# Weight sums on VectorE at each turn's begin, and another order for putting the half-size results together

## The chip, the cores and the metric

One Trainium2 chip, one core. The metric is the device time of one execution in microseconds (us). Engines: PE (TensorE), DVE (VectorE), ACT (ScalarE), POOL (GpSimd), SP (SyncE, which issues the loads).

## The reference

Two transformer blocks of two layers each over 512 tokens of width 1024, in float32. Most of the time goes to six gated feed-forward networks (FFN) of hidden width 2816:

```python
def swiglu(h, w_gate, w_up, w_down):
    return (jax.nn.silu(h @ w_gate) * (h @ w_up)) @ w_down
x = x + 0.5 * swiglu(rms_norm(x, ffn1_norm[l]), ffn1_w_gate[l], ffn1_w_up[l], ffn1_w_down[l])
```

Between them lie convolutions, sparse attention, attention on a memory, retention and differential attention, which the change doesn't touch.

## The kernel before

Activations lie transposed: 128 channels on the partitions, 512 tokens along them. A float32 product is made of three passes over rounded halves: each weight tile `raw` (128x1024, one tile of 128 output columns) is rounded by ACT to `w_hi` (`round_weights`, line 1080) and DVE writes the rest to `w_lo` (`rest_of_weights`, line 1537); the activations are `u_hi` and `u_lo`, the hidden ones `h_hi` and `h_lo`. Weight tiles have running numbers and four slots; bank `n % 4` of PSUM takes tile n. SP loads a tile when the `w_lo` of the tile four before it is written (semaphore `split`), in the order of the numbers. `taken` counts tiles whose bank has been read by DVE.

An FFN (`ffn` of each engine) goes through its 22 hidden tiles in three groups of 8, 8 and 6 (`F_GROUPS`). A group computes gate and up tiles, then a down stage of eight tiles multiplies the group's hidden tiles into the residual. The gate and up work runs in turns of two hidden tiles. In a turn the first pair (tiles n and n+1) is plain: gate scaled by `rstd` (line 1643), tanh on ACT, up scaled (line 1647), (1 + tanh) times gate (line 1650), the product (line 1651), `h_hi` on ACT, `h_lo` on DVE (line 1541).

The second pair (n+2, n+3) is "quick" in 57 turns: the 2x2 block product of (gate, up) by (256-token halves) is made by a Winograd scheme with seven half-size products instead of eight, each 12 matmuls of 256 columns (`fast_pair`, line 588). Its products are m1, m2 (plain weights), then m5, m6, m3, m7 with weight sums S1, S2, S4, S3, and m4. The sums are made in `w_sum` from `raw` of n+2 and n+3 by POOL (`fast_sums`, line 2257), rounded by ACT to `sum_hi` (line 1123, 128x2048) and the rest written by DVE to `sum_lo` (`rest_of_sums`, line 1601). The token sums T1 to T4 are made once for an FFN by DVE (`summed`, lines 1609 to 1617). ACT copies m1 and m5 to `kept`; DVE puts the gate tile together in `fast_gate` (m2 and m3 plus `kept`, then m6 and m1 as `part_2` onto the second half) and the up tile in `fast_up`, from `part_3` (m7 plus `part_2`), `kept` and m4. Each tile is scaled by `rstd`.

Semaphores that matter: `s_made` counts sets of weight sums (ACT's rounding and SP's load of tile n+2 of the next turn, line 444, wait for it), `s_rounded` and `s_split` follow `sum_hi` and `sum_lo`, `w_mm` counts the four sum products of a pair (`w_mm` 5 to 8 of a turn), `f_ready` the `h_lo` tiles. POOL makes the sums of a turn in the turn before, behind `s_split` of that turn. `chain.done` makes an engine wait for its own instruction. The order of DVE's and ACT's work within a turn is the order of the calls in the loop (lines 1698 to 1712 and 1117 to 1137).

In the first FFN the first group is plain throughout. In the other five, the first group has three quick turns after a plain one, in which the norm of the tokens (`norm_scale`), the token sums and their splitting are made too.

Of the kernel before, what the change touches and what calls it, by code (L numbers as in the profile page):

```python
# [29 lines left out]
ALU = mybir.AluOpType  # L30
# [9 lines left out]
RING = 4  # L40
# [168 lines left out]
def two_blocks(nc, A, out):  # L209
    ctx = ExitStack()  # L210
    with ctx:
# [309 lines left out]
        def _(pe):  # L521
# [57 lines left out]
            def product(o, w, rhs):  # L579

                for k in range(KT // 2):
                    (wh, wl), (rh, rl) = w(k), rhs(k)
                    mm(o, wh, rh, start=k == 0, stop=False)  # L583
                    mm(o, wh, rl, start=False, stop=False)  # L584
                    ins = mm(o, wl, rh, start=False, stop=k == KT // 2 - 1)  # L585
                return ins

            def fast_pair(p, m, fast):
# [25 lines left out]
                product(m5, summed_w(S1), summed_u(T1)).then_inc(w_mm, 1)  # L614
                product(m6, summed_w(S2), summed_u(T2)).then_inc(w_mm, 1)
                product(m3, summed_w(S4), plain_u(1, 1)).then_inc(w_mm, 1)
# [913 lines left out]
        def _(v):  # L1530
# [66 lines left out]

            def rest_of_sums(m):

                v.wait_ge(s_rounded, m + 1)  # L1600
                tt(sum_lo[:, :], w_sum, f32(sum_hi[:, :]), ALU.subtract).then_inc(s_split, 1)  # L1601
# [32 lines left out]
            def ffn(n, q, f, gain, factor, more=True):  # L1634

                for g, (f0, fn) in enumerate(F_GROUPS):
# [19 lines left out]
                    def fast_gate(p, m, f_at):  # L1656
                        v.wait_ge(w_kept, m + 1)
                        v.wait_ge(w_mm, m * 4 + 6)
                        tt(part_2, bank[RING][:, 0:HS], kept[:, 0:HS], ALU.add)
                        v.wait_ge(f_ready, F_TILES * f + f_at)  # L1660
                        v.wait_ge(w_mm, m * 4 + 7)
                        chain.done(v, tt(gate_t, bank[p.plus(1).slot][:, :], kept, ALU.add))
                        chain.done(v, tt(gate_t[:, HS:S], gate_t[:, HS:S], part_2, ALU.add))
                        tt(gate_t, gate_t, rstd[:, :], ALU.mult).then_inc(taken, 1)

                    def fast_up(p, m, f_at, h_at):
                        v.wait_ge(w_mm, m * 4 + 8)
                        chain.done(v, tt(part_3, bank[RING + 1][:, 0:HS], part_2, ALU.add))
                        stt(up_t[:, HS:S], part_3, -1.0, kept[:, HS:S], ALU.mult, ALU.subtract)
                        v.wait_ge(tiles, p.no + 1)  # L1670
                        chain.done(v, stt(up_t[:, 0:HS], part_3, -1.0, bank[RING + 2][:, 0:HS], ALU.mult, ALU.subtract))
                        tt(up_t, up_t, rstd[:, :], ALU.mult).then_inc(taken, 1)
                        v.wait_ge(f_tanh, F_TILES * f + f_at + 1)
                        chain.done(v, stt(gate_t, tanh_t, 1.0, gate_t, ALU.add, ALU.mult))
                        tt(gate_t, gate_t, up_t, ALU.mult).then_inc(f_prod, 1)
                        rest_of_weights(p)
                        v.wait_ge(f_rounded, F_TILES * f + f_at + 1)
                        rest(tile(h_hi, h_at), tile(h_lo, h_at), gate_t, 1.0, f_ready)
# [19 lines left out]
                    with chain.loop(v, 1 if g == 0 else 0, fn // 2, 2 if fast is None else 6) as i:  # L1698
# [5 lines left out]
                        else:  # L1704
                            m = i + (FAST_PAIRS * fast + FAST_AT[g])
                            gate(At(n, i), i * 2 + f0)
# [515 lines left out]
        def _(pool):  # L2222
# [34 lines left out]
            def fast_sums(n, q):  # L2257

                fast = FAST[q]
                pool.wait_ge(stat_diag, q + 1)  # L2260

                def part(j):
                    return w_sum[:, j * HC:(j + 1) * HC]

                for g, (f0, fn) in enumerate(F_GROUPS):
                    if quick(q, g) is None:
                        n = n + 2 * fn + 8
                        continue
                    with chain.loop(pool, 1 if g == 0 else 0, fn // 2, 2) as i:
                        p, m = At(n + 2, i), i + (FAST_PAIRS * fast + FAST_AT[g])  # L2270
                        p1 = p.plus(1)
                        a11, a12 = raw[:, p.slot, 0:HC], raw[:, p.slot, HC:CH]
                        a21, a22 = raw[:, p1.slot, 0:HC], raw[:, p1.slot, HC:CH]
                        pool.wait_ge(s_split, m + 1)
                        pool.wait_ge(raw_in[p.slot], (p.turn + 1) * 16)
                        pool.wait_ge(raw_in[p1.slot], (p1.turn + 1) * 16)
                        tt(part(S3), a11, a21, ALU.add)  # L2277
                        chain.done(pool, tt(part(S1), a21, a22, ALU.add))
                        chain.done(pool, tt(part(S2), part(S1), a11, ALU.add))
                        tt(part(S4), part(S2), a12, ALU.add).then_inc(s_made, 1)  # L2280
                    n = n + 2 * fn + 8

# [7 lines left out]
            for l in range(2):  # L2290
                L = L1_AT[l]
                turned = from_slot(L + O_OUT)
                fast_sums(L, 4 * l)
# [40 lines left out]
                fast_sums(L + O_FFN2, 4 * l + 3)  # L2334
# [3 lines left out]
            for l in range(2):  # L2338
# [16 lines left out]
                fast_sums(L + O2_FFN, 9 + 2 * l)  # L2355
# [36 lines left out]
```

## Time and profile before

| | us |
|---|---|
| median of 3 runs (lowest, highest) | 3489.7 (3488.18, 3491.91) |
| the profiled execution, its own time | 3487.0 |
| its span, first to last instruction | 3485.2 |
| PE busy, of the span | 3432.3 (98%) |
| DVE busy | 2421.6 (69%) |
| ACT busy | 1407.1 (40%) |
| POOL busy | 959.5 (28%) |

Busy time is the time in which an engine has an instruction in work. A row of the timeline gives start, duration, engine, line, operation and what is written and read; in brackets stands how long the engine was idle before it and what released it. Matmuls overlap, so that their starts, not their durations, give the pace. The granted clock (PEclk) is a share of 2.4 GHz.

### The profile page before, as it was taken

What the parts mean: (1) busy time and instruction counts of PE and PEld (TensorE: products, weight loads), DVE (VectorE), ACT (ScalarE), POOL (GpSimd) and SP (SyncE); (2) the same over time, 40 slices, a digit from 0 to 9 for tenths busy, and PEclk for the clock granted to TensorE, in tenths of its full rate; (3) what the DMA queues carried; (4) which work ended last, traced back from release to release, by engine and by line L of the source; (5) the groups of instructions that cost most, each with busy time, mean ns of one, the idle gap of its engine ahead of it and who ended that gap; (6) DMA issues with size and microseconds to landing.
All of it is one profiled execution on the core that took longest, in us unless ns stands there. A gap on an engine that the chain in (4) does not pass through costs nothing.

```text
span 3485.2 us, 51264 instructions
## 1 busy us (share of the span) xinstructions
PE 3432.3 (98%) x18454; PEld 2863.7 (82%) x18454; DVE 2421.6 (69%) x3375; ACT 1407.1 (40%) x2163; POOL 959.5 (28%) x631
## 2 busy tenths in 40 slices
PE   8999999999999999999999999999999999999998
PEld 7888786878888888878687888887888888888887
DVE  6677897468567967779756856765696585567755
ACT  4333365344334433336534433434443343443333
POOL 0112394123112411239412311230322130041213
PEclk9999999999999999999999999999999999999999
DMA  5332432423333333243242333331233333223331
GB/s 159 97 99 88 104 103 67 115 79 91 103 97 90 97 103 98 87 106 103 67 115 80 91 102 97 91 91 55 85 96 97 97 95 86 61 73 108 97 97 61
DMA packets 621280, 324.65 MB, mean 93 GB/s; under 512 B 13488, under 2 KB 616520, under 8 KB 621128
## 3 DMA queue, kind: packets, MB, share of 16 engines
q1 hardware_dynamic: 617096, 317.15, 31.4%
q10 hardware_dynamic: 4032, 5.51, 0.7%
q8 instruction: 91, 1.49, 0.2%
q14 instruction: 61, 0.50, 0.0%
HBM read 314.75 MB, written 2.10 MB: 91 GB/s over the span
## 4 chain that ended last, share of the span: by engine, by line
PE 85%; DVE 6%; issue 5%; ACT 2%; POOL 2%; DMA 0%; ACTq 0%; SPq 0%; DVEq 0%; POOLq 0%
PE bank L544 20%; PE bank L542 20%; PE bank L543 20%; PE bank L583 5%; PE bank L585 5%; PE bank L584 5%; PE bank L696 1%; POOL mem L2310 1%; PE bank L698 1%; PE bank L697 1%; DVE w_lo L1537 1%; PE bank L682 1%; PE bank L900 1%; PE bank L884 1%; PE bank L936 1%
## 5 line engine op out<-in xcount | busy, mean ns | idle before, releaser
L1080 ACT ACTIVATE w_hi<-raw 128x1024 fp32r<-128x1024 f32 x602 | 635.3, 1058 | 1193.3 <-PE bank L544 1181.0
L1537 DVE TENSOR_TENSOR w_lo<-raw,w_hi 128x1024 fp32r<-128x1024 f32 x602 | 838.8, 1395 | 203.0 <-ACT w_hi L1080 202.7
L544 PE MATMUL bank<-u_hi,w_lo 128*128 128x512 f32 x1920 | 763.6, 398 | 0.0
L542 PE MATMUL bank<-u_hi,w_hi 128*128 128x512 f32 x1920 | 761.1, 396 | 1.9 <-DVE mem L1546 1.5
L543 PE MATMUL bank<-u_lo,w_hi 128*128 128x512 f32 x1920 | 756.5, 394 | 0.0
L542 PE MATMUL bank<-h_hi,w_hi 128*128 128x512 f32 (+1 forms) x1568 | 605.9, 386 | 5.6 <-DVE h_lo L1541 4.9
L544 PE MATMUL bank<-h_hi,w_lo 128*128 128x512 f32 (+1 forms) x1568 | 608.9, 388 | 0.0
L543 PE MATMUL bank<-h_lo,w_hi 128*128 128x512 f32 (+1 forms) x1568 | 603.3, 385 | 0.0
L2277 POOL TENSOR_TENSOR mem<-raw 128x512 f32<-128x512 f32 x57 | 105.8, 1855 | 1335.0 <-DMA raw<-in_ffn_w_up 540.3
L542 PEld LDWEIGHTS bank<-u_hi,w_hi 128*128 128x128 f32 x1920 | 360.5, 188 | 91.9 <-issue 6.7
L543 PEld LDWEIGHTS bank<-u_lo,w_hi 128*128 128x128 f32 x1920 | 360.6, 188 | 87.0
L544 PEld LDWEIGHTS bank<-u_hi,w_lo 128*128 128x128 f32 x1920 | 360.4, 188 | 85.2
L1627 DVE SCALAR_TENSOR_TENSOR x<-bank,x 128x512 f32 (+1 forms) x192 | 132.4, 689 | 374.0 <-PE bank L544 373.9
L542 PEld LDWEIGHTS bank<-h_hi,w_hi 128*128 128x128 f32 x1568 | 294.3, 188 | 72.7 <-DVE h_lo L1541 7.5
L543 PEld LDWEIGHTS bank<-h_lo,w_hi 128*128 128x128 f32 x1568 | 294.6, 188 | 67.4 <-issue 0.5
L544 PEld LDWEIGHTS bank<-h_hi,w_lo 128*128 128x128 f32 x1568 | 294.5, 188 | 63.7
L2310 POOL TENSOR_TENSOR mem<-mem,spare 128x512 f32<-128x512 f32 x120 | 169.4, 1446 | 106.9 <-ACT spare L1302 106.5
L583 PE MATMUL bank<-t_hi,sum_hi 128*128 128x256 f32 x684 | 190.4, 278 | 3.4 <-DVE sum_lo L1601 3.4
L584 PE MATMUL bank<-t_lo,sum_hi 128*128 128x256 f32 x684 | 189.4, 277 | 0.0
L585 PE MATMUL bank<-t_hi,sum_lo 128*128 128x256 f32 x684 | 189.3, 277 | 0.0
L2229 POOL TENSOR_TENSOR mem<-mem 128x512 f32<-128x512 f32 x95 | 174.1, 1833 | 7.4
L2228 POOL TENSOR_TENSOR mem<-x 128x512 f32 (+1 forms) x95 | 136.4, 1435 | 87.5 <-DVE x L1627 74.9
(300 smaller groups left out, 5722.1 us busy)
## 6 DMA issues: line engine op xcount, KB each, us to landing
raw<-in_w_in SPq DMA_DIRECT2D x96, 512.0 KB, 3.8
raw<-in_ffn_w_gate SPq DMA_DIRECT2D x88, 512.0 KB, 3.9
raw<-in_ffn_w_up SPq DMA_DIRECT2D x88, 512.0 KB, 3.8
raw<-in_ffn_w_down SPq DMA_DIRECT2D x64, 512.0 KB, 3.9
raw<-in_w_gate SPq DMA_DIRECT2D x44, 512.0 KB, 3.9
raw<-in_w_up SPq DMA_DIRECT2D x44, 512.0 KB, 3.8
raw<-in_w_out SPq DMA_DIRECT2D x32, 512.0 KB, 4.1
raw<-in_xa_wkv SPq DMA_DIRECT2D x32, 512.0 KB, 4.0
```

The source lines that it names most:

```text
L542: mm(o, w_hi[:, s, w], rhs_hi[:, r], start=k == order[0], stop=False)
L543: mm(o, w_hi[:, s, w], rhs_lo[:, r], start=False, stop=False)
L544: ins = mm(o, w_lo[:, s, w], rhs_hi[:, r], start=False, stop=k == order[-1])
L583: mm(o, wh, rh, start=k == 0, stop=False)
L584: mm(o, wh, rl, start=False, stop=False)
L585: ins = mm(o, wl, rh, start=False, stop=k == KT // 2 - 1)
L1080: a(w_hi[:, p.slot, :], raw[:, p.slot, :], ACT.Copy).then_inc(rounded, 1)
L1537: tt(w_lo[:, p.slot, :], raw[:, p.slot, :], f32(w_hi[:, p.slot, :]), ALU.subtract).then_inc(split, 1)
L1627: stt(tile(x, k), bank[p.slot][:, :], factor, tile(x, k), ALU.mult, ALU.add).then_inc(taken, 1)
L2228: chain.done(pool, tt(square, tile(x, k), tile(x, k), ALU.mult))
L2229: tt(sumsq, sumsq, square, ALU.add).then_inc(sq_sum, 1)
L2310: tt(conv[n % 2], conv[n % 2], tap_t[n % 4], ALU.add).then_inc(tap_added, 1)
```

## The change

POOL's `fast_sums` and its three calls go. DVE gets `weight_sums` with the same four additions, called as the first thing of each quick turn, behind waits for the two loads; it signals `s_made` as before. PE makes m3 before m6. In `fast_gate` the wait for `f_ready` comes first, then the full-width addition (after m3), then `part_2` (after m6). In `fast_up` the up tile isn't scaled by `rstd` any more; instead (1 + tanh) times gate is. The first half of the up tile, which needs m4, is written after that, releases the banks, and DVE waits for it before the last product.

```diff
--- before.py
+++ after.py
@@ -612,8 +612,8 @@
                 pe.wait_ge(t_split, T_COUNT * (fast + 1))
                 pe.wait_ge(s_split, m + 2)
                 product(m5, summed_w(S1), summed_u(T1)).then_inc(w_mm, 1)
+                product(m3, summed_w(S4), plain_u(1, 1)).then_inc(w_mm, 1)
                 product(m6, summed_w(S2), summed_u(T2)).then_inc(w_mm, 1)
-                product(m3, summed_w(S4), plain_u(1, 1)).then_inc(w_mm, 1)
                 product(m7, summed_w(S3), summed_u(T3)).then_inc(w_mm, 1)
                 pe.wait_ge(split, p1.no + RING + 1)
                 product(m4, plain_w(p1.slot, 1), summed_u(T4)).then_inc(tiles, 1)
@@ -1595,6 +1595,19 @@
                 v.wait_ge(u_rounded, k + 8 * q + 1)
                 rest(tile(u_hi, k), tile(u_lo, k), tile(x, k), col(gain), u_ready)
 
+            def weight_sums(p, m):
+
+                p1 = p.plus(1)
+                s1, s3, s2, s4 = (w_sum[:, j * HC:(j + 1) * HC] for j in range(4))
+                a11, a12 = raw[:, p.slot, 0:HC], raw[:, p.slot, HC:CH]
+                a21, a22 = raw[:, p1.slot, 0:HC], raw[:, p1.slot, HC:CH]
+                v.wait_ge(raw_in[p.slot], (p.turn + 1) * 16)
+                v.wait_ge(raw_in[p1.slot], (p1.turn + 1) * 16)
+                tt(s3, a11, a21, ALU.add)
+                chain.done(v, tt(s1, a21, a22, ALU.add))
+                chain.done(v, tt(s2, s1, a11, ALU.add))
+                tt(s4, s2, a12, ALU.add).then_inc(s_made, 1)
+
             def rest_of_sums(m):
 
                 v.wait_ge(s_rounded, m + 1)
@@ -1655,11 +1668,11 @@
 
                     def fast_gate(p, m, f_at):
                         v.wait_ge(w_kept, m + 1)
+                        v.wait_ge(f_ready, F_TILES * f + f_at)
                         v.wait_ge(w_mm, m * 4 + 6)
-                        tt(part_2, bank[RING][:, 0:HS], kept[:, 0:HS], ALU.add)
-                        v.wait_ge(f_ready, F_TILES * f + f_at)
+                        tt(gate_t, bank[p.plus(1).slot][:, :], kept, ALU.add)
                         v.wait_ge(w_mm, m * 4 + 7)
-                        chain.done(v, tt(gate_t, bank[p.plus(1).slot][:, :], kept, ALU.add))
+                        chain.done(v, tt(part_2, bank[RING][:, 0:HS], kept[:, 0:HS], ALU.add))
                         chain.done(v, tt(gate_t[:, HS:S], gate_t[:, HS:S], part_2, ALU.add))
                         tt(gate_t, gate_t, rstd[:, :], ALU.mult).then_inc(taken, 1)
 
@@ -1667,11 +1680,13 @@
                         v.wait_ge(w_mm, m * 4 + 8)
                         chain.done(v, tt(part_3, bank[RING + 1][:, 0:HS], part_2, ALU.add))
                         stt(up_t[:, HS:S], part_3, -1.0, kept[:, HS:S], ALU.mult, ALU.subtract)
-                        v.wait_ge(tiles, p.no + 1)
-                        chain.done(v, stt(up_t[:, 0:HS], part_3, -1.0, bank[RING + 2][:, 0:HS], ALU.mult, ALU.subtract))
-                        tt(up_t, up_t, rstd[:, :], ALU.mult).then_inc(taken, 1)
                         v.wait_ge(f_tanh, F_TILES * f + f_at + 1)
                         chain.done(v, stt(gate_t, tanh_t, 1.0, gate_t, ALU.add, ALU.mult))
+                        tt(gate_t, gate_t, rstd[:, :], ALU.mult)
+                        v.wait_ge(tiles, p.no + 1)
+                        ins = stt(up_t[:, 0:HS], part_3, -1.0, bank[RING + 2][:, 0:HS], ALU.mult, ALU.subtract)
+                        ins.then_inc(taken, 1)
+                        v.wait_ge(taken, p.no + RING + 1)
                         tt(gate_t, gate_t, up_t, ALU.mult).then_inc(f_prod, 1)
                         rest_of_weights(p)
                         v.wait_ge(f_rounded, F_TILES * f + f_at + 1)
@@ -1695,7 +1710,7 @@
                         if not q:
                             tables()
                         up(At(n + 3), 1, 1)
-                    with chain.loop(v, 1 if g == 0 else 0, fn // 2, 2 if fast is None else 6) as i:
+                    with chain.loop(v, 1 if g == 0 else 0, fn // 2, 2 if fast is None else 7) as i:
                         if fast is None:
                             for jj in range(2):
                                 rest_of_weights(At(n + 2 * jj, i))
@@ -1703,6 +1718,7 @@
                                 up(At(n + 2 * jj + 1, i), i * 2 + (f0 + jj), i * 2 + jj)
                         else:
                             m = i + (FAST_PAIRS * fast + FAST_AT[g])
+                            weight_sums(At(n + 2, i), m)
                             gate(At(n, i), i * 2 + f0)
                             rest_of_sums(m)
                             rest_of_weights(At(n, i))
@@ -2254,32 +2270,6 @@
                     chain.done(pool, tt(j_inv, j_var, minus_half[:, 0:NQ], ALU.pow))
                 tt(inv, var, minus_half[:, 0:NQ], ALU.pow).then_inc(stat_inv, 1)
 
-            def fast_sums(n, q):
-
-                fast = FAST[q]
-                pool.wait_ge(stat_diag, q + 1)
-
-                def part(j):
-                    return w_sum[:, j * HC:(j + 1) * HC]
-
-                for g, (f0, fn) in enumerate(F_GROUPS):
-                    if quick(q, g) is None:
-                        n = n + 2 * fn + 8
-                        continue
-                    with chain.loop(pool, 1 if g == 0 else 0, fn // 2, 2) as i:
-                        p, m = At(n + 2, i), i + (FAST_PAIRS * fast + FAST_AT[g])
-                        p1 = p.plus(1)
-                        a11, a12 = raw[:, p.slot, 0:HC], raw[:, p.slot, HC:CH]
-                        a21, a22 = raw[:, p1.slot, 0:HC], raw[:, p1.slot, HC:CH]
-                        pool.wait_ge(s_split, m + 1)
-                        pool.wait_ge(raw_in[p.slot], (p.turn + 1) * 16)
-                        pool.wait_ge(raw_in[p1.slot], (p1.turn + 1) * 16)
-                        tt(part(S3), a11, a21, ALU.add)
-                        chain.done(pool, tt(part(S1), a21, a22, ALU.add))
-                        chain.done(pool, tt(part(S2), part(S1), a11, ALU.add))
-                        tt(part(S4), part(S2), a12, ALU.add).then_inc(s_made, 1)
-                    n = n + 2 * fn + 8
-
             nc.gpsimd.memset(par_in[:, 2 * P:3 * P], 0.0).then_inc(pool_set, 1)
             nc.gpsimd.memset(minus_half, -0.5).then_inc(pool_set, 1)
             nc.gpsimd.memset(half_pi, math.pi / 2).then_inc(pool_set, 1)
@@ -2290,7 +2280,6 @@
             for l in range(2):
                 L = L1_AT[l]
                 turned = from_slot(L + O_OUT)
-                fast_sums(L, 4 * l)
                 squares(L + N_FFN - 8, 4 * l + 1)
...
```

## Rows read from the trace of the kernel before

**Rows 1.** The page, busy time of each engine over the whole span.

```profile
PE 3432.3 (98%) x18454; PEld 2863.7 (82%) x18454; DVE 2421.6 (69%) x3375; ACT 1407.1 (40%) x2163; POOL 959.5 (28%) x631
```

**Rows 2.** Waits of PE, whole span: us in total, times, longest.

```profile
PE bank L542 <- DVE h_lo L1541: 4.9, 6, 0.8
...
PE bank L583 <- DVE sum_lo L1601: 3.4, 5, 0.8
```

**Rows 3.** Timeline of DVE, one steady turn of the second group.

```profile
950.62 0.69 DVE L1643 TENSOR_TENSOR mem<-bank,rstd 128x512 f32<-128x512 f32 x1 [1.32 <-PE bank L544]
...
956.22 0.69 DVE L1647 TENSOR_TENSOR mem<-bank,rstd 128x512 f32<-128x512 f32 x1 [1.57 <-PE bank L544]
...
971.63 0.69 DVE L1643 TENSOR_TENSOR mem<-bank,rstd 128x512 f32<-128x512 f32 x1 [1.33 <-PE bank L544]
```

**Rows 4.** Timeline of PE, first sum product and third down stage.

```profile
829.93 0.39 PE L583 MATMUL bank<-t_hi,sum_hi 128*128 128x256 f32 x1 [0.84 <-DVE sum_lo L1601]
...
1120.16 0.50 PE L542 MATMUL bank<-h_hi,w_hi 128*128 128x512 f32 x1 [0.80 <-DVE h_lo L1541]
```

**Rows 5.** Timeline of DVE, start of the second FFN.

```profile
803.71 2.20 DVE L1612 TENSOR_TENSOR sums<-sums 128x1024 f32<-128x1024 f32 x1
...
810.29 0.68 DVE L1643 TENSOR_TENSOR mem<-bank,rstd 128x512 f32<-128x512 f32 x1
...
826.95 0.69 DVE L1643 TENSOR_TENSOR mem<-bank,rstd 128x512 f32<-128x512 f32 x1
827.59 2.29 DVE L1601 TENSOR_TENSOR sum_lo<-mem,sum_hi 128x2048 fp32r<-128x2048 f32 x1
```

**Rows 6.** Timeline of ACT, rounding of the sums and of tile n+2.

```profile
825.64 1.91 ACT L1123 ACTIVATE sum_hi<-mem 128x2048 fp32r<-128x2048 f32 x1
...
959.96 1.05 ACT L1080 ACTIVATE w_hi<-raw 128x1024 fp32r<-128x1024 f32 x1
```

**Rows 7.** Timeline of DVE, last quick turn of the third group.

```profile
1113.11 0.69 DVE L1662 TENSOR_TENSOR mem<-bank,mem 128x512 f32<-128x512 f32 x1 [1.00 <-PE bank L585]
...
1117.67 0.69 DVE L1675 TENSOR_TENSOR mem<-mem 128x512 f32<-128x512 f32 x1
1118.29 1.22 DVE L1537 TENSOR_TENSOR w_lo<-raw,w_hi 128x1024 fp32r<-128x1024 f32 x1
1119.42 0.68 DVE L1541 SCALAR_TENSOR_TENSOR h_lo<-mem,h_hi 128x512 f32 x1
```

**Rows 8.** Line 1612, all six: ns min, median, max; first, last start.

```profile
L1612 DVE TENSOR_TENSOR sums<-sums x6: 1219/2204/2210, 131.5 to 3120.7; 128x1024 f32<-128x1024 f32 x6
```

**Rows 9.** Busy by stretch: length; PE, PEld, DVE, ACT, POOL; PEclk; DMA share; GB/s.

```profile
802.40:812.00 9.60, 9.60 (x43) 7.74 (x42) 9.43 (x8) 2.54 (x4) 8.42 (x4) 1.00 0.01 3
```

**Rows 10.** Timeline of DVE, second and third quick turn of the second FFN.

```profile
847.43 2.29 DVE L1601 TENSOR_TENSOR sum_lo<-mem,sum_hi 128x2048 fp32r<-128x2048 f32 x1
...
850.77 0.69 DVE L1647 TENSOR_TENSOR mem<-bank,rstd 128x512 f32<-128x512 f32 x1
...
852.59 1.66 DVE L1651 TENSOR_TENSOR mem<-mem 128x512 f32<-128x512 f32 x1
...
859.26 0.41 DVE L1659 TENSOR_TENSOR mem<-bank,mem 128x256 f32<-128x256 f32 x1
...
866.52 0.69 DVE L1643 TENSOR_TENSOR mem<-bank,rstd 128x512 f32<-128x512 f32 x1
867.27 2.29 DVE L1601 TENSOR_TENSOR sum_lo<-mem,sum_hi 128x2048 fp32r<-128x2048 f32 x1
...
875.52 0.42 DVE L1659 TENSOR_TENSOR mem<-bank,mem 128x256 f32<-128x256 f32 x1
```

**Rows 11.** Tile raw, 820 to 1010: time from issue to landing.

```profile
DMA to landing us min/median/max: 3.6/4.0/5.3
```

**Rows 12.** Busy by stretch, as rows 9, in the attention of block one.

```profile
564.00:568.00 4.00, 2.48 (x9) 1.29 (x11) 3.93 (x13) 3.09 (x10) 0.00 (x0) 0.75 0.15 44
568.00:572.00 4.00, 4.00 (x21) 2.36 (x18) 3.02 (x7) 3.28 (x8) 0.00 (x0) 0.82 0.32 95
```

More of the change, by code:

```diff
@@ L2333, in _ @@
                 norm_inv(4 * l + 3)
-                fast_sums(L + O_FFN2, 4 * l + 3)
                 squares(L + O_FFN2 + N_FFN - 8, 4 * l + 4)
@@ L2354, in _ @@
                 norm_inv(9 + 2 * l)
-                fast_sums(L + O2_FFN, 9 + 2 * l)
                 if l:
```

## The prediction

> **What bounds the kernel now.** I read the busy shares first: PE is busy 98% of the span [rows 1]. Then the waits of PE, because only what PE waits for can be won, and only a new wait of PE can be lost. The change touches two of them: the first sum product of an FFN waits for `sum_lo` (5 times, 3.4 us), and a down stage waits for the last `h_lo` (6 times, 4.9 us) [rows 2]. The reader is to see how small they are: a turn of the quick loops costs PE 21.01 us (the same gate eviction starts at 950.62 and at 971.63), and there DVE waits for PE (1.33 us), not PE for DVE [rows 3]. So 57 steady turns can't get faster, and the change is worth what it does at 5 starts and 6 ends.
>
> **The start of an FFN (5 times: every quick FFN but the first).** PE's first sum product starts at 829.93 after 0.84 us idle, released by `sum_lo` [rows 4]. `sum_lo` (2.29 us from 827.59) had waited for ACT's `sum_hi` (825.64 + 1.91 = 827.55, a hop of 0.04) [rows 5, 6]. DVE has been working without a gap since the norm: it, not POOL, is the path.
> - Added on the path: four adds of 128x512 from SBUF to SBUF. One takes 0.69 without POOL beside it [rows 7]. The first isn't chained, and the next op then starts 0.64 later (826.95 to 827.59 [rows 5]); two are chained (0.72 each); the last ends after 0.69: 2.77. And ACT's rounding, which now runs beside DVE's own work because POOL made the sums early, comes in series: hop 0.04, 1.91, hop 0.04. From the end of the second tile's work to `sum_lo` that is 4.76, where it was 0.64: +4.12.
> - Removed from the path: POOL's adds beside DVE. Three token sums of 128x1024 take from 803.71 to the gate at 810.29, 6.58 [rows 5]. The one such sum that never met POOL took 1.22 [rows 8]; an op of that length that isn't chained lets the next one start after 1.13 (1118.29 to 1119.42 [rows 7]), so two at 1.13 and one chained at 1.26 make 3.52. Relief 3.06. Everything behind (tanh, `t_hi`, `t_lo`, the second tile) is a gapless chain on DVE and ACT and moves up by it: PE's tiles were done long before.
> - Net +4.12 - 3.06 = +1.06 each, idle 0.84 becoming 1.9; times 5 is +5.3 us. Bounds: relief nothing, +4.12 each; relief as large as what is added, 0 each; and below that the present wait with its restart (the first product then takes 0.39 [rows 4]), about -1 each. I take 1.06, since both halves are rows of this very stretch.
>
> What slows DVE there? Over 802.40 to 812.00 the DMA engines are 1% busy and POOL 8.42 of 9.6 us [rows 9], so it is POOL. Beside POOL an add with both inputs in SBUF takes 1.66 (852.59), an eviction with a PSUM input 0.69 (850.77) [rows 10]. The Trainium skill (SBUF — State Buffer, section "SBUF: two separate sides") says that VectorE and GpSimd take a port pair in turn, and that a VectorE op with two SBUF inputs is held only against a GpSimd op that reads SBUF. By that rule, which the rows bear out, the relief comes in full and the new adds, though of the kind that can be held, find nothing on POOL. Without the rule one could not tell whether the relief comes, and the sum at a start would lie anywhere from +1.06 to +4.12.
>
> **The next turns of that first group (2 in each of the 5).** DVE isn't waiting there either: `sum_lo` to `sum_lo` is 19.84 (847.43 to 867.27) [rows 10], below PE's 21.01, so it catches up. The stretch from `sum_lo` to the results takes 11.83 beside POOL (847.43 to 859.26) and 8.25 without (867.27 to 875.52): relief 3.58. The rest up to the gate is 7.26 (859.26 to 866.52) and keeps it: same ops in another order. New turn: 8.25 + 7.26 + 2.77 + 0.04 + 1.91 + 0.04 = 20.27. That fits under 21.01 by 0.74. Priced at nothing; the cover is that 0.74, and each us above it costs 10 us in all.
>
> **Steady turns.** `h_lo` of the last turn ends 1.33 before the gate at 971.63, so at 970.30 [rows 3]. The sums then take 970.3 to 973.1; the gate starts 1.5 late, which nobody waits for (its bank is next written a turn later); `sum_hi` ends at 975.1 and `sum_lo` at 977.4. A full tile takes PE 5.60 (950.62 to 956.22 [rows 3]), so of the turn 9.8 are left for seven half products of 1.4. PE needs `sum_lo` after one more tile and two products: 971.63 + 5.6 + 2.8 = 980.0. Cover 2.6. Behind `sum_hi` on ACT stand the rounding of tile n and the tanh; both end before the next tile's result at 977.2. Nothing.
>
> **The loads.** SP's wait for `s_made` stands before the load of tile n+2 of the next turn; behind it are queued n+3 and then the pair after. POOL released it in the turn before; now DVE does at 973.1. Landing takes 4.0 median, 5.3 at most [rows 11]; ACT rounds that tile at 959.96 + 21.01 = 980.97 [rows 6]. Landed by 978.4: cover 2.6. Nothing.
>
> **The results and PE's new order.** m3 before m6 lets the gate's full-width add start a product (1.4 us) earlier, at 1111.7 where it was 1113.11 [rows 7]. PE's total is the same. After m4, DVE had four ops: half `up`, rstd, (1 + tanh), product; the product ended at 1117.67 + 0.69 = 1118.36 [rows 7]. Now it has the half `up` and the product after m4, but what precedes them hangs on m6, done at 1113.1 as m3 was: three half-size ops and gate times rstd to the third product's sum at 1114.64, half `up` 1115.09, (1 + tanh) 1115.44, rstd 1116.16, last half 1116.77, product 1117.22 to 1117.91. So 0.45 earlier, not the 1.4 that the removed ops suggest: DVE is full from m6 on. In steady turns this is hidden. At the end of the third group PE waits for the last `h_lo` (0.80; it starts at 1120.16, `h_lo` ends at 1120.10) [rows 4, 7]: 6 x -0.45 = -2.7 us. Bounds 0 and the whole wait with its restart, about -1 each. The first two groups end with eight tiles in the down stage and don't wait.
>
> **Sum.** +5.3 - 2.7 = +2.6 us. The profiled execution took 3487.0 (span 3485.2 and 1.8 around it): 3489.6. The median of the runs is 2.7 above that, so 3492.3 against 3489.7.
>
> **Rivals.**
> - *The clock falls in the longer wait (slower).* Where PE, on small matmuls, stood still for 1.5 of 4 us, the granted clock was 0.75 of 2.4 GHz there and 0.82 in the next 4 us: 2.0 and 1.4 us at the level of 1.2 GHz, 1.7 us lost [rows 12]. My wait of 1.9 is longer. Against: it stands between dense matmuls, and that stretch did not. Price 5 x 1.7 = 8.5: 3500.8. It decides if one wait of 1.9 at the first sum product is enough; its place is there and nowhere else.
> - *The relief doesn't come.* DVE stays as slow as now: +15.3 at the starts, and turns of 23.85 instead of 21.01, +28.4: 3536. A smaller failure, above 0.74 of the 3.58, begins to show at some us.
> - *The loads land late*, more than 2.6 us beyond the rows: each further us up to 50 us.
> - *The waits vanish (faster).* The starts come a little earlier than now instead of later and the ends lose their whole wait: 3.4 + 4.9 [rows 2] and eleven restarts of 0.2 (estimated from the 0.39 and 0.50 of the first products [rows 4]) are 10.5: 3479.2. It needs 2 us more relief at each start than I find, and twice the gain at the ends.
> - *Nothing visible*, the two terms cancelling: 3489.7. This lies within the forecast's range.
>
> **Chances.** Forecast (3487 to 3497, cancelling included) 0.68; clock 0.13; relief partial or absent 0.06; loads or another wait 0.03; waits vanish wholly or mostly 0.10. Range 3484 to 3501: it takes in the clock case. About 0.2% (7 us) is what a measurement of this kernel can tell from no change. Faster by more 0.09; within 0.71; slower by more 0.20.
>
> **What would show it.** `L1614` and its neighbours at 1.2 us and no POOL in quick turns; PE's wait for `sum_lo` 5 times with some 1.9 us each, all at starts; the wait for `h_lo` down to some 0.35 six times; steady turns still 21.01 apart; SP waiting for the last sum, ACT never for a load. A granted clock below 1.00 right after a start speaks for the first rival, `sum_lo` waits 15 times for the second. The prediction is wrong if PE waits in steady turns at all.

## The result, and the profile after

| us | before | after |
|---|---|---|
| median (lowest to highest of 20 runs each) | 3489.9 (3487.65 to 3492.13) | 3494.59 (3492.2 to 3498.33) |
| ratio, with its 95% interval | | 1.0014 (1.0008 to 1.002) |
| the profiled execution, its own time | 3487.0 | 3493.1 |
| its span | 3485.2 | 3491.3 |

The kernel became 4.7 us slower, 0.14%; 2.6 were forecast. By the bound of 0.2% that is no change; it lies within the range (3484 to 3501) and within the forecast's own (3487 to 3497). The interval of the ratio is +2.8 to +7.0 us.

The page of after, its busy times. POOL went from 959.5 to 569.3; DVE gained only 25, though 57 turns of four additions at 0.69 are 157: with POOL out of its way its own instructions are shorter.

```profile
PE 3438.1 (98%) x18454; PEld 2868.5 (82%) x18454; DVE 2446.8 (70%) x3603; ACT 1410.8 (40%) x2163; POOL 569.3 (16%) x403
```

The waits of PE in after (us in total, times, longest), which answer to [rows 2]: the five at the starts grew from 3.4 to 8.0, the six at the ends shrank from 4.9 to 2.1. Five and six, as before, so no wait appeared in a steady turn.

```profile
PE bank L583 <- DVE sum_lo L1614: 8.0, 5, 1.8
...
PE bank L542 <- DVE h_lo L1541: 2.1, 6, 0.4
```

DVE in after, at the start of the second FFN and on through its three quick turns, which answers to [rows 5] and [rows 10]:

```profile
804.51 1.23 DVE L1625 TENSOR_TENSOR sums<-sums 128x1024 f32<-128x1024 f32 x1
...
808.04 0.68 DVE L1656 TENSOR_TENSOR mem<-bank,rstd 128x512 f32<-128x512 f32 x1
...
824.49 0.69 DVE L1606 TENSOR_TENSOR mem<-raw 128x512 f32<-128x512 f32 x1
...
827.15 0.68 DVE L1656 TENSOR_TENSOR mem<-bank,rstd 128x512 f32<-128x512 f32 x1
829.32 2.29 DVE L1614 TENSOR_TENSOR sum_lo<-mem,sum_hi 128x2048 fp32r<-128x2048 f32 x1 [1.49 <-ACT sum_hi L1123]
...
849.43 2.29 DVE L1614 TENSOR_TENSOR sum_lo<-mem,sum_hi 128x2048 fp32r<-128x2048 f32 x1 [1.49 <-ACT sum_hi L1123]
...
869.55 2.29 DVE L1614 TENSOR_TENSOR sum_lo<-mem,sum_hi 128x2048 fp32r<-128x2048 f32 x1 [1.49 <-ACT sum_hi L1123]
```

Token sums take 1.23 instead of the slowed ones of before; three of them up to the gate take 808.04 - 804.51 = 3.53. From the first added sum to `sum_lo` it is 829.32 - 824.49 = 4.83. The two turns behind the start are 20.11 and 20.12 apart, under PE's 21.01. In the bracket of `sum_lo` DVE now waits 1.49 for ACT's `sum_hi`: that is the rounding that POOL's early sums had let run beside DVE's own work.

PE in after, at the same place and at the end of that FFN's third group (against [rows 4]: 0.84 and 0.80):

```profile
831.66 0.39 PE L583 MATMUL bank<-t_hi,sum_hi 128*128 128x256 f32 x1 [1.78 <-DVE sum_lo L1614]
...
1121.50 0.50 PE L542 MATMUL bank<-h_hi,w_hi 128*128 128x512 f32 x1 [0.36 <-DVE h_lo L1541]
```

To see where the span grew, I took the starts of the same matmul in both traces (18454 in each, in the same order) and looked for the places at which their difference jumps. A jump at a start or an end is taken from the matmul before the place to the 60th behind it. Times are those of before:

| place | jumps, us | sum |
|---|---|---|
| five starts (829.93, 1189.45, 1963.22, 2556.92, 3146.91) | +0.99, +0.91, +0.87, +0.83, +0.97 | +4.6 |
| six ends (346.60, 1120.16, 1479.69, 2253.55, 2847.28, 3437.14) | -0.45, -0.45, -0.46, -0.44, -0.46, -0.44 | -2.7 |
| the first 17 us, before any turn | +2.1 | +2.1 |
| one exchange of halves (1540.27) and attention (548 to 572, 1660 to 1710) | +0.8, -1.0, +1.9 | +1.7 |

Together 5.7 of the span's 6.1. The first two lines are the change's, +1.9 together (the expectations below have them from a coarser reading, +4.8 and -2.75). The others lie where the two kernels run the same instructions. In the attention they go with the clock: over 550 to 580 and 1660 to 1715 us the granted clock is 0.94 and 0.91 in before, 1.00 and 0.84 in after. The jump of the first 17 us (1.5 to 3.3 us) also came in nine of the twelve other profiles below against this one of before, those of before's neighbours too (not in `again`, `sums_only_2` and `pool_writes`), so here it is the profile of before that was a short one: its run took 3487.0 where the median is 3489.9.

That leaves a question. The profiles give the change +1.9; the medians, 20 runs each, give 4.7. Where are the other 2.8?

### The profile page after: what moved, and what is told of

Same layout as the page of the kernel before. It is cut to its first block, busy times and chain, and to the rows that moved or that the text cites. A ratio compares the mean times of both kernels' runs of the same rounds, so it can differ in the third digit from the quotient of the medians.

```text
span 3491.3 us, 51074 instructions
## 1 busy us (share of the span) xinstructions
PE 3438.1 (98%) x18454; PEld 2868.5 (82%) x18454; DVE 2446.8 (70%) x3603; ACT 1410.8 (40%) x2163; POOL 569.3 (16%) x403
## 3 DMA queue, kind: packets, MB, share of 16 engines
q8 instruction: 91, 1.49, 0.2%
## 4 chain that ended last, share of the span: by engine, by line
PE 86%; DVE 6%; issue 3%; ACT 2%; POOL 1%; DMA 0%; ACTq 0%; DVEq 0%; SPq 0%; POOLq 0%
PE bank L544 20%; PE bank L542 20%; PE bank L543 20%; PE bank L583 5%; PE bank L585 5%; PE bank L584 5%; PE bank L696 1%; PE bank L698 1%; PE bank L697 1%; DVE w_lo L1537 1%; PE bank L682 1%; PE bank L900 1%; POOL mem L2299 1%; PE bank L884 1%; PE bank L936 1%
## 5 line engine op out<-in xcount | busy, mean ns | idle before, releaser
L1537 DVE TENSOR_TENSOR w_lo<-raw,w_hi 128x1024 fp32r<-128x1024 f32 x602 | 787.0, 1309 | 202.5 <-ACT w_hi L1080 201.6
L1123 ACT ACTIVATE sum_hi<-mem 128x2048 fp32r<-128x2048 f32 x57 | 109.8, 1926 | 217.5 <-DVE mem L1609 217.5
L1614 DVE TENSOR_TENSOR sum_lo<-mem,sum_hi 128x2048 fp32r<-128x2048 f32 x57 | 130.7, 2293 | 76.2 <-ACT sum_hi L1123 76.2
```

Source lines behind the costliest of these rows:

```text
L1123: a(sum_hi[:, :], w_sum, ACT.Copy).then_inc(s_rounded, 1)
L1537: tt(w_lo[:, p.slot, :], raw[:, p.slot, :], f32(w_hi[:, p.slot, :]), ALU.subtract).then_inc(split, 1)
```

## The experiments

My theory: each start costs one wait longer by 0.92 to 0.94, each end gives 0.45 back, and that is all. Rivals: the clock falls in the longer wait, in those executions that weren't profiled; some part of the change costs elsewhere.

### The same kernel again, and each half alone

`again`, and later `again_2` and `again_3`, are the changed kernel without an edit. `results_only` is before with the new order of results alone, `fast_gate` and `fast_up` as in after (POOL keeps the sums):

```diff
-                product(m6, summed_w(S2), summed_u(T2)).then_inc(w_mm, 1)
                 product(m3, summed_w(S4), plain_u(1, 1)).then_inc(w_mm, 1)
+                product(m6, summed_w(S2), summed_u(T2)).then_inc(w_mm, 1)
...
```

`sums_only` is before with the sums on VectorE alone, in the old order of results:

```diff
+                            weight_sums(At(n + 2, i), m)
                             gate(At(n, i), i * 2 + f0)
...
-                fast_sums(L, 4 * l)
```

> The changed kernel once more, with a second profile. Theory A: the change is worth +4.8 us at the five starts (wait for sum_lo 0.84 to 1.78) and -2.75 at the six ends (wait for h_lo 0.81 to 0.36), +2.05 together, and what the first profile showed beyond it (+2.1 in the first 17 us, +0.8 at a wait of L757 on an exchange of halves, +0.9 net in the stretches at the lower clock of the two attentions) is a matter of the single execution: it differs in this profile, while the five and the six steps come again. Rival B: these steps are the change's too, and come again with the same sizes.

> Only the other order of the results (m3 before m6, rstd on (1 + tanh) times gate); the weight sums stay with POOL. Theory A: the ends gain 0.45 each, the starts keep their 0.84 of wait: 6 x -0.45 = -2.7, 0.9992 of the kernel before. Rival: DVE is as full as before beside POOL, m3's earliness finds no DVE that is free, and the gain at the ends is 0 (1.0000).

> Only the weight sums on DVE at each turn's begin; the results in the old order. Theory A: +0.95 at each of five starts, ends unchanged (0.8 of wait): +4.8 us, 1.0014. Rival: the turns behind a start have a cycle of DVE that no longer fits under PE's 21.01 us in the old order, and PE waits for sum_lo up to 15 times: +10 us and more, 1.003.

| kernel | median, us | against before (3489.45) | expected |
|---|---|---|---|
| again | 3494.06 | +4.6 (ratio 1.0004 to 1.0022) | |
| results_only | 3487.22 | -2.2 (0.9984 to 1.0002) | -2.7 |
| sums_only | 3497.9 | +8.4 (1.0014 to 1.0032) | +4.8 |

The results' order does what its row says, as far as the medians can tell (the interval, -5.6 to +0.7 us, takes in no change). Its waits of PE show it:

```profile
PE bank L583 <- DVE sum_lo L1601: 3.5, 5, 0.9
...
PE bank L542 <- DVE h_lo L1541: 2.2, 6, 0.4
```

The sums cost 3.6 more than the expected 4.8, which was their waits. In the profile of `sums_only` the waits for `sum_lo` are those of after (8.0, 5 times, 1.8 the longest), yet its jumps at the first three starts are +2.54, +2.53 and +2.43, not 0.9 to 1.0. Windows of 10 us at each of the first four starts of `sums_only` (window: us, PE, PEld, DVE, ACT, POOL busy, granted clock, DMA share, GB/s):

```profile
830.00:840.00 10.00, 8.24 (x58) 8.03 (x57) 9.21 (x10) 5.17 (x7) 0.00 (x0) 0.83 0.70 199
1192.00:1202.00 10.00, 8.24 (x57) 8.04 (x56) 9.19 (x10) 5.22 (x7) 0.00 (x0) 0.83 0.70 196
1970.00:1980.00 10.00, 8.23 (x57) 8.03 (x56) 9.82 (x12) 4.51 (x7) 0.00 (x0) 0.83 0.68 194
2567.00:2577.00 10.00, 8.62 (x68) 8.25 (x68) 9.85 (x14) 3.96 (x7) 0.00 (x0) 1.00 0.56 162
```

A granted clock of 0.83 over 10 us is 3.4 us at the lower level, 1.2 GHz: half the clock for 3.4 us loses 1.7, at the first three starts. At the fourth (2568.48), whose wait is shorter (1.38), it stays 1.00. So the first rival is at work, in part. The kernel of after does the same in some executions: `again` shows it at two of these three starts.

```profile
828.00:838.00 10.00, 8.23 (x57) 8.03 (x56) 9.58 (x11) 4.78 (x7) 0.00 (x0) 0.83 0.72 204
1190.00:1200.00 10.00, 8.24 (x68) 7.90 (x67) 9.89 (x12) 4.34 (x6) 0.00 (x0) 1.00 0.67 190
1966.00:1976.00 10.00, 8.61 (x60) 8.61 (x61) 9.85 (x14) 3.97 (x6) 0.00 (x0) 0.83 0.57 161
```

The wait before it was no longer than in after, where the clock stayed at 1.00. First the start in `again`, then the 4 us behind it in `again`, then the same 4 us in after:

```profile
830.68 0.39 PE L583 MATMUL bank<-t_hi,sum_hi 128*128 128x256 f32 x1 [1.77 <-DVE sum_lo L1614]
```

```profile
832.00:836.00 4.00, 4.00 (x23) 4.00 (x23) 3.95 (x6) 2.06 (x3) 0.00 (x0) 0.57 0.45 134
```

```profile
832.00:836.00 4.00, 4.00 (x37) 4.00 (x36) 3.97 (x6) 1.19 (x2) 0.00 (x0) 1.00 0.51 146
```

23 matmuls where 37 fit. The jumps in `again` at its two falls are +2.49 and +2.45: 1.5 to 1.6 more than at the same starts without a fall.

### POOL given back to the starts: one that reads SBUF, one that only writes

Does the relief of 3.06 per start come from POOL's reading, and what does a much longer wait do to the clock? Both kernels are after with unused work on POOL behind the same norm that had started its sums, at the five starts; everything is computed as in after.

```diff
+            def beside(q):
+                pool.wait_ge(stat_diag, q + 1)
+                a, b = const[:, C_DIST:C_DIST + S], const[:, C_NEG:C_NEG + S]
+                for j in range(4):
+                    chain.done(pool, tt(view(12800, S), a, b, ALU.add))
```

`pool_writes` has ten memsets there instead:

```diff
+                for j in range(10):
+                    chain.done(pool, nc.gpsimd.memset(view(12800, S), 0.0))
```

> The changed kernel with four additions of 128x512 added on POOL behind the norm, where POOL made its first weight sums before; they read constants in SBUF, and their result is used nowhere. Theory A (POOL's reads slow DVE ops with two SBUF inputs): the token sums take 2.2 again instead of 1.22, a start is later by 3.06, and the wait for sum_lo goes from 1.78 to about 4.8 at each start (15 us in all); so long a wait brings the clock down at each. Rival B (the token sums were slow for another reason): they stay at 1.22, the wait at 1.78.

> As the one before, but POOL fills a tile with zeros ten times (128x512, no input) instead of adding. By the rule of the Trainium skill (SBUF - State Buffer, section SBUF: two separate sides) an op of VectorE with two SBUF inputs is held only against a GpSimd op that reads SBUF. Theory A, with the rule: the token sums stay at 1.22, the wait at 1.78. Rival B (any use of SBUF by POOL holds them): some 2 us for each token sum, the wait some 3 us longer. Besides, five more starts at the wait of 1.78: by the count so far (5 of 15 at which the clock fell behind the wait, a step of 2.2 to 2.6 us instead of 0.95) one or two of the five.

> The changed kernel, a third profile. Theory C (the first rival of the prediction, in part): behind a wait of 1.78 the clock falls in some executions and not in others, at 2 us more than without; 1 or 2 of the first three starts, never the last two (wait 1.34). Theory D (the two starts seen with it were chance of another kind): none.

Measured, one run each, before being 3488.56: `pool_reads` 3520.4, `pool_writes` 3490.97, `again_2` 3488.59. POOL and DVE at the second FFN's start in `pool_reads`:

```profile
806.39 8.93 POOL L2278 TENSOR_TENSOR mem<-const 128x512 f32<-128x512 f32 x4 [2.17 <-DVE diag_lo L1571]
```

```profile
807.48 2.20 DVE L1625 TENSOR_TENSOR sums<-sums 128x1024 f32<-128x1024 f32 x1
809.61 2.31 DVE L1627 TENSOR_TENSOR sums<-sums 128x1024 f32<-128x1024 f32 x1
```

and in `pool_writes`:

```profile
801.13 5.78 POOL L2277 MEMSET mem<- 128x512 f32 x10 [2.15 <-DVE diag_lo L1571]
```

```profile
802.24 1.23 DVE L1625 TENSOR_TENSOR sums<-sums 128x1024 f32<-128x1024 f32 x1
804.64 1.23 DVE L1630 TENSOR_TENSOR sums<-sums 128x1024 f32<-128x1024 f32 x1
```

POOL is busy across the token sums in both; 2.20 and 2.31 beside its adds, 1.23 beside its memsets. So a busy POOL isn't enough to hold DVE: its additions do, its memsets, which write SBUF without reading it, don't. That the reading makes the difference, and not something else in which an addition differs from a memset, these two kernels alone don't show. The Trainium skill (SBUF — State Buffer, section "SBUF: two separate sides") says that it is the reading: a VectorE instruction with two SBUF inputs is held only against a GpSimd instruction that reads SBUF. These two kernels agree with it.

The adds bring back the 3.06 that was counted as relief, and more. PE's waits for `sum_lo` in `pool_reads`:

```profile
PE bank L583 <- DVE sum_lo L1614: 23.2, 5, 4.8
```

4.8 is the 1.78 of after and 3.06 (4.4 at the last two starts). But the jumps against before are +6.25, +6.29, +6.48, +5.37 and +6.51, where 0.9 + 3.06 is 4.0: the clock is down behind all five. Over 14 us at each start it is 0.76, and 0.88 at the fourth: 6.7 us at 1.2 GHz at four of them, 3.4 at the fourth. In `pool_reads`:

```profile
836.00:840.00 4.00, 2.33 (x11) 2.33 (x12) 3.97 (x5) 1.70 (x3) 0.00 (x0) 0.50 0.67 176
```

`pool_writes` adds three starts with a wait of 1.75 to 1.77, not the five of its expectation (its last two wait 1.34 and 1.35); the clock fell at one.

### What of the new order makes the ends shorter

`m3_only` is before with m3 before m6 and `fast_gate` in the new order; `rstd_only` is before with the new `fast_up` alone:

```diff
-                        tt(up_t, up_t, rstd[:, :], ALU.mult).then_inc(taken, 1)
+                        tt(gate_t, gate_t, rstd[:, :], ALU.mult)
+                        v.wait_ge(tiles, p.no + 1)
+                        ins = stt(up_t[:, 0:HS], part_3, -1.0, bank[RING + 2][:, 0:HS], ALU.mult, ALU.subtract)
+                        ins.then_inc(taken, 1)
```

> The kernel before with m3 before m6 and the full-width gate addition ahead of part_2; rstd still scales the up tile. The working of the prediction: behind m4 the same four ops as before hang on m4 itself, so the ends gain nothing: wait for h_lo 0.8 six times. Rival: m3's earliness moves the whole tail, wait 0.36.

> The kernel before with rstd on (1 + tanh) times gate; m6 still before m3. The working: the tail then hangs on m3, which comes third as m6 does in the changed kernel, but behind it stand the full-width addition and one half-size op more: h_lo some 0.2 earlier, the wait 0.8 to 0.6. Rival: this move alone makes the whole gain, wait 0.36, and the order of the products is idle.

> The changed kernel, a fourth profile, for the count of starts at which the clock falls. Theory C: so far 3 of 12 at waits of 1.76 to 1.78 in four profiles with these waits in this order of the results (0, 2, 0, 1 of 3), none at 1.34: 0 to 2 of the first three starts here, a step of 2.2 to 2.6 where it falls, 0.8 to 1.0 where not.

> The weight sums alone on DVE, a second profile. In the first the clock fell at all of the first three starts. Theory C (chance of the execution): it need not here; the kernel's starts are the changed kernel's. Rival: the old order of the results makes it fall each time, and that is why this kernel is 8.4 us slower than the one before and not 4.8: 3 of 3 again.

One run each (before 3489.96): `m3_only` 3489.74, `rstd_only` 3487.46, `again_3` 3490.03, `sums_only_2` 3495.87. The waits are the finer measure. First `m3_only`, then `rstd_only`:

```profile
PE bank L542 <- DVE h_lo L1541: 4.8, 6, 0.8
```

```profile
PE bank L542 <- DVE h_lo L1541: 3.6, 6, 0.6
```

m3 first is worth nothing alone: the up tile's first half stands behind m4, and so does all that follows. DVE in `m3_only`:

```profile
1118.43 0.42 DVE L1671 SCALAR_TENSOR_TENSOR mem<-mem,bank 128x256 f32<-128x256 f32 x1 [0.36 <-PE bank L585]
```

The scale moved ahead of m4 takes 0.2 off each end; both together 0.45. In `rstd_only` nothing waits for m4 any more, and what decides is the full-width addition that hangs on m3:

```profile
1114.53 0.69 DVE L1662 TENSOR_TENSOR mem<-bank,mem 128x512 f32<-128x512 f32 x1 [1.00 <-PE bank L585]
```

From there to `h_lo` DVE has no gap. With m3 ahead of m6 that addition is made in the gap, and only half-size work is left behind. So the products' new order has an effect only where the move of the scale has cleared the way behind m4. The two executions themselves (-0.2 and -2.5 against a single run) couldn't show that; the waits do.

### A version without the wait

DVE has a gap at each start: in after it waits 1.76 at 813.74 for ACT's `h_hi` of the first hidden tile. The sums of the first turn fit in there, if the loads have come. `early_sums` makes them in `up` of that tile and takes the first turn out of the loop:

```diff
                         rest_of_weights(p)
+                        if between is not None:
+                            between()
                         v.wait_ge(f_rounded, F_TILES * f + f_at + 1)
...
-                        up(At(n + 1), 0, 0)
+                        m1 = 1 + FAST_PAIRS * (fast or 0) + FAST_AT[0]
+                        up(At(n + 1), 0, 0, (lambda: weight_sums(At(n + 2, 1), m1)) if fast is not None else None)
```

> The changed kernel, but the sums of the first quick turn after a norm are made earlier: in the place where DVE waits 1.76 us for ACT's h_hi of the first tile (before L1541 at 813.74). Theory A (at a start the change lost by putting sum_hi in series and won by taking POOL away): the adds fill the wait and cost some 1.0, sum_hi runs beside DVE again, sum_lo ends some 3 us earlier than in the changed kernel, and the five waits are gone: 8.0 us and five restarts of 0.2, so -9 against the changed kernel, -4.3 - 2.75 = -7 against the one before, 0.9980 (or 0.9987 if the unexplained part stays). Rival (the path of a start is ACT's, not DVE's): the waits stay above 1 us and the kernel stays at 1.001.

The median is 3481.53, 7.9 below before (0.9967 to 0.9987; -7 was expected) and 12.5 below `again` (-9). DVE in `early_sums`, and then ACT:

```profile
814.01 0.68 DVE L1606 TENSOR_TENSOR mem<-raw 128x512 f32<-128x512 f32 x1
...
816.67 0.69 DVE L1541 SCALAR_TENSOR_TENSOR h_lo<-mem,h_hi 128x512 fp32r<-128x512 f32 x1
...
828.27 2.29 DVE L1614 TENSOR_TENSOR sum_lo<-mem,sum_hi 128x2048 fp32r<-128x2048 f32 x1
```

```profile
826.33 1.91 ACT L1123 ACTIVATE sum_hi<-mem 128x2048 fp32r<-128x2048 f32 x1
```

No bracket stands behind `h_lo` or `sum_lo`: the sums fill the gap, `sum_hi` follows `h_hi` at once, and DVE no longer waits for it. PE's waits have no row for `sum_lo` at all; the jumps against before are -1.08, -1.09, -1.20, -0.79 and -0.72 at the starts and -0.44 to -0.46 at the ends, -7.6 in all. The five starts lose their wait (0.83 to 0.84, and 0.42 and 0.46) and 0.24 to 0.37 of restart with it. No wait is left at a start, the clock fell at none, and the median (-7.9) and the jumps (-7.6) agree, which they did not in after.

The profile as a whole doesn't show the gain: its span is 3484.4, only 0.8 below before's, and its run (3486.18) is the longest of the nine. The other 6.8 lie outside the change: 1.9 in the first 20 us, and most of the rest where the clock was lower than in before's profile (0.89 over 515 to 530 us against 1.00, 0.84 over 1660 to 1715 against 0.91). The clock thus moves single executions by some us at other places too, and a profile has to be read place by place.

That leaves the ends' 0.36. `h_lo_first` is `early_sums` with the last `h_lo` ahead of the `w_lo` in `fast_up`:

```diff
-                        rest_of_weights(p)
                         v.wait_ge(f_rounded, F_TILES * f + f_at + 1)
                         rest(tile(h_hi, h_at), tile(h_lo, h_at), gate_t, 1.0, f_ready)
+                        rest_of_weights(p)
```

> The kernel with the early sums, and in the up tile's tail h_lo is written before the next weights' rest instead of after it. Theory A (the end of a third group is the chain product, h_hi on ACT 0.63, h_lo on DVE): h_lo starts 0.45 earlier (behind h_hi, not behind the 1.13 of the rest), the six waits of 0.36 go: -2.8 us against the early sums, 0.9969 of the kernel before. Rival: DVE's cycle in the turns behind a start grows by the 0.68 it now waits for h_hi, from 20.1 to 20.8, and with the rest of the weights later PE waits in a turn: no gain, or a loss of some us.

The median is 3483.49, 5.1 below before's 3488.56 (0.9977 to 0.9995); that it lies above `early_sums` is not clear of the intervals, but the wait is longer, not gone. The waits and DVE at the end of the second FFN's third group:

```profile
PE bank L542 <- DVE h_lo L1541: 3.0, 6, 0.5
```

```profile
1113.36 0.41 DVE L1677 TENSOR_TENSOR mem<-bank,mem 128x256 f32<-128x256 f32 x1
...
1117.44 0.69 DVE L1692 TENSOR_TENSOR mem<-mem 128x512 f32<-128x512 f32 x1
1119.08 0.69 DVE L1541 SCALAR_TENSOR_TENSOR h_lo<-mem,h_hi 128x512 f32 x1 [0.94 <-ACT h_hi L1137]
```

The product starts at 1117.44 and `h_lo` 1.64 later; with `w_lo` (1.13) between them, as in after, it is 1120.76 - 1119.01 = 1.75. Only 0.1 is won. I had counted on more: behind the product's 0.69 come ACT's 0.63 and two hops, which I took at 0.04 each; they are 0.15 and 0.17 here, and `w_lo` had hidden them. The 0.94 for which DVE now idles comes in every turn and moves the rest of its turn back: at m6 it has no gap left (no bracket at 1113.36, where after has 0.69 at 1114.91), so the product itself starts later against PE. What was won behind the product is more than lost ahead of it: the wait grew by 0.14.

### How often the clock falls

Whether the clock fell behind a start can be told by the jump: at waits of 1.73 to 1.78 it is 0.8 to 1.0 without, 2.4 to 2.6 with.

| wait before the first product | kernels | falls |
|---|---|---|
| 0.40 to 0.86 (all five) | before, results_only, m3_only, rstd_only | 0 of 20 |
| 1.33 to 1.38 (last two starts) | after, again (4 in all), pool_writes, sums_only (2) | 0 of 14 |
| 1.73 to 1.78 (first three) | after, again (4 in all), pool_writes | 3 of 15 |
| 1.73 to 1.78 (first three) | sums_only (2) | 5 of 6 |
| 4.38 to 4.80 (all five) | pool_reads | 5 of 5 |

The second profile of `sums_only` has both outcomes in itself. Behind its third start, where the jump is +0.92:

```profile
1970.00:1980.00 10.00, 9.28 (x70) 8.86 (x71) 9.81 (x16) 3.96 (x6) 0.00 (x0) 1.00 0.50 138
```

For `sums_only` this closes the sum: 4.6 for the waits and 5/6 of three falls of 1.5 are 8.4, as measured. For after it doesn't close: 1.9 and 3/15 of three falls are 2.8, against 4.7 measured, at the edge of the interval (2.8 to 7.0). Some 1.9 us stay open. If they are falls at the starts, it takes 1.9 in an execution where the profiles show 0.6; five profiles are too few to exclude that (one of them had two), but I haven't shown it.

Every run also lists its mean granted clock, and what an execution lost to the clock, anywhere, can be estimated from it: the share below 1 times 3490 us. The mean of the 31 runs of before beside `again` is 0.99552; of the 11 of `again` 0.99509, of `sums_only` 0.99418, of `results_only` 0.99536, of the 9 of `early_sums` 0.99544. That is 1.5, 4.7, 0.6 and 0.3 us lost more than in before, each give or take 0.7 to 0.9 by the scatter of the runs. With the jumps without falls it makes +3.4, +9.3, -2.1 and -7.3, where +4.6, +8.4, -2.2 and -7.9 were measured. So the clock may be a larger part of what was missing in after than the count says; some 1.2 us are left, which the scatter can hold. Where these falls lie can't be read from a mean. The single executions point the same way: `again_2` and `again_3`, without a fall at a start and with 1.00 and 0.94 in the attention, took 3488.59 and 3490.03 beside 3488.56 and 3489.96 of before.

Open, too, is why the old order of results should have a fall nearly each time and the new one seldom, at waits of the same length.

## Why the prediction was right, and where its sum was off

The number fell inside the forecast, but not by its sum alone: of the measured 4.7 the two terms of the sum make 1.9, the clock at least a part of the rest, and the width of the forecast (10 us) took in what the sum had left out. What follows is where the single steps held.

- **The starts' wait.** Forecast 1.9 each; 1.78, 1.75, 1.75, 1.34 and 1.38. What a start costs was forecast at +1.06, and is +0.83 to +0.99. Its two halves: the series of adds and rounding 4.76, measured 4.83 (the hop into `sum_hi` is 0.14, not 0.04: the last add ends at 826.54 + 0.69 = 827.23, and the rounding starts at 827.37); three token sums 3.52, measured 3.53. The stretch between the two, which the sum had left as it was, got 0.2 shorter (826.95 - 810.29 = 16.66 before, 824.49 - 808.04 = 16.45 in after), and so +1.06 became +0.94 of wait. The adds had to be priced from rows of other operations of the same kind and shape and the relief from one row that had never met POOL; both held to 0.1 at the second FFN's start.
- **The turns behind a start.** Forecast 20.27, measured 20.11; PE never waits there. Steady turns are still 21.01 apart. The two rows of after, `sum_lo` starting at 976.3 as against the 975.1 forecast:

```profile
955.31 2.29 DVE L1614 TENSOR_TENSOR sum_lo<-mem,sum_hi 128x2048 fp32r<-128x2048 f32 x1 [1.49 <-ACT sum_hi L1123]
...
976.32 2.29 DVE L1614 TENSOR_TENSOR sum_lo<-mem,sum_hi 128x2048 fp32r<-128x2048 f32 x1 [1.49 <-ACT sum_hi L1123]
```

- **The loads.** SP issued the load at 974.26, forecast 973.1. Both differences are less than the 1.7 by which after stands later here as a whole, so the stage is some 0.5 earlier in its turn than forecast. ACT waits for a load once in the whole span, 7.1 us, in before as in after.

```profile
974.26 0.37 SPq L436 DMA_DIRECT2D raw<-in_ffn_w_gate  x1
```

- **The ends.** Forecast -0.45 each, measured -0.44 to -0.46, -2.7 in all, as in the sum. The reason given, DVE full from m6 on, is the bracket of `part_2`, after which no other stands up to `h_lo`:

```profile
1114.91 0.42 DVE L1675 TENSOR_TENSOR mem<-bank,mem 128x256 f32<-128x256 f32 x1 [0.69 <-PE bank L585]
...
1119.01 0.69 DVE L1690 TENSOR_TENSOR mem<-mem 128x512 f32<-128x512 f32 x1
...
1120.76 0.68 DVE L1541 SCALAR_TENSOR_TENSOR h_lo<-mem,h_hi 128x512 f32 x1
```

- **The step that was mis-sized is the clock's.** The prediction treated it as all or nothing: either no start loses any (the forecast) or all five lose 1.7 (the rival, 3500.8). In its place the runs showed a fall in some executions, at the first three starts only, worth about 1.5. Its share in after is 0.9 us by the profiles (3 of 15), 1.5 by the mean clock of the runs (all places), and at most the 2.8 by which the medians exceed the jumps. The forecast's +2.6 was near the +1.9 of the profile without falls; the median has them in it. The last two starts had shown the way in [rows 2]: five waits of 3.4 us in all, 0.8 the longest, can't all be 0.8. The prediction took one start for five, which cost nothing in its sum but hid that two of the five have waits too short for the rival.
- **The other rivals fell.** The relief came in full, no load was late, no wait vanished by itself; it took `early_sums` to make the five vanish.

## What to carry to other kernels

Work taken from a lightly used engine and given to the one that feeds the critical product costs its whole time where that engine has no gap (here 4.19 at a start, of which 3.05 came back because POOL no longer held DVE), even if the steady state has room for it; look for a gap of the receiving engine a little earlier and put the first piece there, as `early_sums` does. Price a wait of TensorE with what it may do to the granted clock behind it, as a cost that comes in some executions only, and judge it by medians of many runs together with several profiles, never by one. Of two reorderings that touch the same tail, try each alone: here one is worth nothing without the other.

## What the runs showed of the hardware

- One wait of TensorE of 1.73 to 1.78 us between dense matmuls was followed by some 3.4 us at 1.2 GHz in 8 of 21 cases, at a cost of 1.5 to 1.6 us; at 1.33 to 1.38 us in 0 of 14, at 0.40 to 0.86 us in 0 of 20; at 4.38 to 4.80 us in 5 of 5, four times with some 6.7 us at 1.2 GHz (2.3 to 2.6 us lost) and once with 3.4 (1.5). The same program differs from one execution to the next.
- Ten chained memsets on POOL (5.78 us) left a VectorE addition of 128x1024 at 1.23 us; chained additions on POOL made it 2.20 to 2.31.
- A hop from one engine to another, from the end of an instruction to the start of the one that waited for it, is not one number: VectorE to ScalarE took 0.14 to 0.15 (the last added sum to `sum_hi` in after, the product to `h_hi` in `h_lo_first`), but 0.03 from the scaled gate of after (820.03 + 0.69) to its tanh (820.75); ScalarE to VectorE took 0.17 behind the `h_hi` in `h_lo_first`, and 0.03 in after both behind the `h_hi` of the first tile (0.61 us, ended at 813.71) and behind the `sum_hi` (1.92 us). What decides it these rows don't show.
- The first 17 us of an execution took 1.5 to 3.3 us longer than in before's profile in ten of the thirteen others, and 0.1 or less in three, with the same instructions there. Between 15 and 20 us 24 matmuls start in before, 17 in after, and 15 in `results_only` with a granted clock of 0.54; in after the profile shows 1.00 there, so that the clock is the cause isn't shown for it.
